# Mixer and expert block: VectorE's turned rows, up's clip and glu put together behind the first low part of the down row

## The chip, the cores and the metric

The kernel is one program on one core of a Trainium2 chip. What is measured is the device time of one execution, in microseconds (us), the median of the runs shown. The core has TensorE (matmuls and transposes through the matrix unit), VectorE (called DVE in the profile), ScalarE (ACT), GpSimd (POOL) and SyncE (SP), which here only issues the loads. Each runs its own list of instructions in order and waits on semaphores for the others.

## The reference

Two blocks stand one behind the other, with 512 tokens of width 1024. The first is a mixer (an mLSTM in chunks and a pooling branch), then a layer of 32 experts, of which each token uses four. The second is a stick-breaking attention with spatial gating. The change touches the experts alone:

```python
logits = (xt @ w_router + b_router).astype(jnp.float32)
top_vals, top_idx = lax.top_k(logits, TOP_K)          # 4 of 32
top_gates = jax.nn.softmax(top_vals, axis=-1)
...
def expert_block(args):
    xb, e = args                                       # rows of one expert
    gate = xb @ w_gate[e] + b_gate[e]                  # 1024 x 1024
    up = xb @ w_up[e] + b_up[e]                        # 1024 x 1024
    gate = jnp.minimum(gate, SWIGLU_LIMIT)             # 7
    up = jnp.clip(up, -SWIGLU_LIMIT, SWIGLU_LIMIT)
    glu = gate * jax.nn.sigmoid(SWIGLU_ALPHA * gate)
    return (glu * (up + 1.0)) @ w_down[e] + b_down[e]  # 1024 x 1024
...
y_buf = y_buf * gate_buf[:, None]
out = jax.ops.segment_sum(y_buf, tok_buf, num_segments=T + 1)[:T]
```

## The kernel before, in words

**Places.** The experts are taken in an order found at run time, one behind the other at 32 places e = 0 to 31. At even places there is room for 128 rows, at odd places (`small(e)`) for 64; what is over would be done in a loop afterwards.

**High and low parts.** Products are kept near float32 by splitting both factors: the high part is the value rounded to the matmul's format, the low part is the rest, and high by high, high by low and low by high are summed. For weights ScalarE writes the high part (`high`, L1062: `WH` from the landing place `ring` or `land`), and VectorE subtracts it from the landed value (`low`, L1408: `low` or `WL`). A low part is written over the place that the weights landed in; ten places are shared so. For the rows of an expert the high parts are `xh` (gathered rows, turned) and `hh` (glu, turned), the low parts `xl` and `hl`. At an odd place the low part lies in the other half of `xh` or `hh`, so that one matmul of 128 columns multiplies both with the high weights, and the lower half of the result is added to the upper one by a fold (L789), after ScalarE has copied it (`egl` for the gate, `eul` L1215 for up, `ysl` for the output).

**Groups.** A matrix of weights comes in four pieces of 1 MB. Each piece is one group of matmuls on TensorE (`rows_by_columns`): 24 matmuls of 512 columns at an even place, 16 at an odd one. There are five buffers for high parts, so ScalarE can make the high part of piece n only when TensorE is done with piece n - 5, and the ten places let SyncE load piece n when TensorE is done with piece n - 10. `ahead(n)` is n + 4: in the step of piece n, ScalarE and VectorE make the parts of piece n + 4.

**What is done at place e, in TensorE's order.** `tensor_gate_up(e)`: four groups of gate and four of up; before the last three of them, behind group 4, comes `tensor_index(e + 3)`, a product of the one-hots of place e + 3 (`oh`, L1703 on VectorE) that gives which rows this expert has. Then `tensor_turn_rows(e + 1)` (L775, `PS<-C,xg`): the gathered rows of the next place are turned into PSUM banks 6 and 7. Then `tensor_down(e - 1)`: the four groups of the down weights of the place before (the down row of this text). Then `tensor_turn_mid(e)` (L775, `PS<-C,eu`): the glu of place e is turned into the same banks 6 and 7. It waits for the glu (`s_eh`) and for the low part of the next rows (`s_tl`), since that reads these banks.

**VectorE at place e.** During gate and up: the low part of the weights in each of eight steps; in step 1 the low part of the glu turned before (`hh` or `hl`); in step 2 the one-hots of place e + 3 (L1703); in step 5 the index of place e + 3 (three short instructions, L1709 to L1713, `iv`, `dst`, `tok`). During the down row: four low parts of weights and three instructions more, `vector_up` (L1730, up's clip, `eu`), `vector_glu` (L1736, (up + 1) times the gate's part, `eu`), and `vector_turn8` (L1720 `xl` or L1718 `xh`, the low part of the next rows). Where these three stand is what the change alters.

**ScalarE at place e.** The high parts of the weights, the high part of the turned rows (`scalar_turn8`, L1206 and L1204), the gate's clip and gelu (L1231, L1233), the copies for the folds and the output `ys` (L1243). GpSimd gathers the rows of place e + 2 and scatters the output of place e - 1; SyncE issues one load of 1 MB a piece.

All of these orders are written out by hand in loops; no planner is at work.

Of the kernel before, what the change touches and what calls it, by code (L numbers as in the profile page):

```python
# [15 lines left out]
T, D, E, K = 512, 1024, 32, 4  # L16
# [57 lines left out]
def program(nc, x, norm1_g, w_in, ig_b, fg_b, conv_w, head_norm_g, pool_w, pool_scale, w_out, norm2_g,  # L74
# [51 lines left out]
    def reg(name, shape, dt, kb):  # L126
        return place(name, shape, dt, off=R0 + int(kb * KB))
# [77 lines left out]
    xh = reg("xh", [128, 8, 128], F32R, 8)  # L205
    xl = reg("xl", [128, 8, 128], F32R, 12)
# [228 lines left out]
    t_rows = {e: max(0, 2 * e - 1) for e in range(E)}  # L435
    t_mid = {e: 2 * e + 2 if e + 1 < E else 2 * e + 1 for e in range(E)}
    NI = 3
    small = lambda e: e % 2 == 1
# [11 lines left out]
    def ahead(n):  # L450
        return n + 2 if n >= second else min(n + NX - 1, second - 1) if n >= first else min(n + 2, first)
# [602 lines left out]
    def high(upto):  # L1054

        while state["hi"] <= min(upto, NP - 1):
            n = state["hi"]
            state["hi"] += 1
            A.wait_ge(s_land[spot[n]], landed(n))
            if before[n]:  # L1060
                A.wait_ge(s_mm, before[n])
            A.activation(WH[buf[n]], lands[spot[n]], ACT.Copy).then_inc(s_hi, 1)  # L1062
# [138 lines left out]
    def scalar_turn8(t, o, e):  # L1201
        A.wait_ge(s_tt, t + 1)
        if small(e):
            A.activation(o[:, :, 0:HALF], PS[:, 6, :].rearrange("p (k t) -> p k t", k=8), ACT.Copy).then_inc(s_th, 1)  # L1204
        else:
            A.activation(o, PS[:, 6:8, :].rearrange("p h (k t) -> p (h k) t", k=4), ACT.Copy).then_inc(s_th, 1)  # L1206

    def scalar_gate_low(e):
        A.wait_ge(s_mm, done[n_g[e] + 4])
        A.wait_ge(s_eh, e)  # L1210
        A.activation(egl[HALF:128], PS[HALF:128, 0:2, :], ACT.Copy).then_inc(s_low, 1)

    def scalar_up_low(e):
        A.wait_ge(s_mm, done[n_g[e] + 8])
        A.activation(eul[HALF:128], PS[HALF:128, 2:4, :], ACT.Copy).then_inc(s_low, 1)  # L1215

    def scalar_out_low(e):
        A.wait_ge(s_mm, done[n_d[e] + 4])
        A.activation(ysl[HALF:128], PS[HALF:128, 4:6, :], ACT.Copy).then_inc(s_low, 1)

    def scalar_gate(e):
        n = places(e)
        if small(e):
            A.wait_ge(s_fold, fold["gate", e])
        else:
            A.wait_ge(s_mm, done[n_g[e] + 4])
        if e:
            A.wait_ge(s_eh, e)
        else:
            A.wait_ge(s_sp, 1)  # L1230
        A.activation(eg[0:n], PS[0:n, 0:2, :], ACT.Relu, scale=-1.0, bias=C[0:n, LIM:LIM + 1]).then_inc(s_eg, 1)  # L1231
        A.wait_ge(s_eg, e + 1)
        A.activation(eg[0:n], eg[0:n], ACT.Gelu_apprx_sigmoid, scale=-1.0, bias=C[0:n, LIM:LIM + 1]).then_inc(s_es, 1)  # L1233

    def scalar_out(e):
        n = places(e)
        if e >= 2:
            A.wait_ge(s_y[e % 2], 16 * (e // 2))
        if small(e):
            A.wait_ge(s_fold, fold["out", e])  # L1240
        else:
            A.wait_ge(s_mm, done[n_d[e] + 4])
        A.activation(ys[e % 2][0:n], PS[0:n, 4:6, :], ACT.Copy).then_inc(s_ys, 1)  # L1243

    def scalar_experts():
        A.wait_ge(s_h2, 64)
        high(first + NX - 1)
        scalar_turn8(0, xh, 0)
        for e in range(E + 1):
            if e < E:  # L1250
                for p in range(8):
                    if p == 0 and small(e) and e >= 3:
                        scalar_out_low(e - 2)
                    if p == 4 and small(e):
                        scalar_gate_low(e)
                    high(ahead(n_g[e] + p))
                    if p == (2 if small(e) else 0) and e >= 2:
                        scalar_out(e - 2)
                    if p == 1 and e:
                        scalar_turn8(t_mid[e - 1], hh, e - 1)  # L1260
                    if p == (6 if small(e) else 4):
                        scalar_gate(e)
                    if p == 6 and e == 1:
                        A.wait_ge(s_spt, 1)
                        A.activation(GtT, PS[0:32, 6, :].rearrange("p (j t) -> p j t", j=4), ACT.Copy).then_inc(s_spk, 1)
            else:
                scalar_out(E - 2)
                scalar_turn8(t_mid[E - 1], hh, E - 1)
            for p in range(4):
                if p == 0 and small(e):  # L1270
                    scalar_up_low(e)
                if e:
                    high(ahead(n_d[e - 1] + p))
                if p == 1 and e + 1 < E:
                    scalar_turn8(t_rows[e + 1], xh, e + 1)
        scalar_out_low(E - 1)
        scalar_out(E - 1)
# [122 lines left out]
    def low(upto):  # L1400

        while state["lo"] <= min(upto, NP - 1):
            n = state["lo"]
            state["lo"] += 1
            V.wait_ge(s_hi, n + 1)
            if second <= n < second + NS:
                V.wait_ge(s_mm, low_free[n])
            V.tensor_tensor(WLn[n], lands[spot[n]], WH[buf[n]].bitcast(F32), SUB).then_inc(s_lo, 1)  # L1408
# [271 lines left out]
    def vector_positions():  # L1680
        V.wait_ge(s_pos, 2)
        V.wait_ge(s_m16, 2)
        V.scalar_tensor_tensor(P1, PS[:, 4, 0:128].rearrange("p (j e) -> p j e", j=4), 1.0, M16, ADD, MUL).then_inc(dv.sem, dv.one())
        V.tensor_copy(cnt, PS[:, 4, 128:160]).then_inc(dv.sem, dv.one())
        V.wait_ge(dv.sem, dv.n)
# [29 lines left out]
    def vector_turn8(t, hi, lo, e):  # L1715
        V.wait_ge(s_th, t + 1)
        if small(e):
            V.tensor_tensor(hi[:, :, HALF:128], PS[:, 6, :].rearrange("p (k t) -> p k t", k=8), hi[:, :, 0:HALF].bitcast(F32), SUB).then_inc(s_tl, 1)  # L1718
            return
        V.tensor_tensor(lo, PS[:, 6:8, :].rearrange("p h (k t) -> p (h k) t", k=4), hi.bitcast(F32), SUB).then_inc(s_tl, 1)  # L1720
# [11 lines left out]
    def vector_glu(e):  # L1732
        V.wait_ge(s_eu, e + 1)
        V.wait_ge(s_es, e + 1)
        n = places(e)
        V.scalar_tensor_tensor(eu[0:n], eu[0:n], 1.0, eg[0:n], ADD, MUL).then_inc(s_eh, 1)  # L1736

    def vector_experts():
        V.wait_ge(s_xg[0], 16)
        low(first + 2)  # L1740
        vector_turn8(0, xh, xl, 0)
        vector_positions()
        for q in range(1, NI):
            vector_one_hot(q)
        low(first + 3)
        vector_further_count()
        V.wait_ge(s_ek, 1)
        V.reciprocal(sm, sm).then_inc(dv.sem, dv.one())
        V.wait_ge(dv.sem, dv.n)
        V.tensor_tensor(GK, GK, sm.unsqueeze(2).broadcast_to([128, 4, 4]), MUL).then_inc(s_gk, 1)  # L1750
        V.wait_ge(s_gk, 1)
        spread_out(Gt, GK).then_inc(s_sp, 1)
        low(first + NX - 1)
        for e in range(E + 1):
            if e < E:
                for p in range(8):
                    if e or p < 7:
                        low(ahead(n_g[e] + p))
                    if e == 0 and p + 1 < NI:
                        vector_index(p + 1, 4 + p)  # L1760
                    if p == 1 and e:
                        vector_turn8(t_mid[e - 1], hh, hl, e - 1)
                    if p == 2 and e + NI < E:
                        vector_one_hot(e + NI)
                    if p == 5 and e + NI < E:
                        vector_index(e + NI, 7)
            else:
                vector_turn8(t_mid[E - 1], hh, hl, E - 1)
            if e == 0:
                vector_turn8(t_rows[1], xh, xl, 1)  # L1770
                vector_up(0)
                vector_glu(0)
                low(ahead(n_g[0] + 7))
                continue
            for p in range(4):
                low(ahead(n_d[e - 1] + p))
                if e < E and p == (1 if small(e) else 0):
                    vector_up(e)
                if e < E and p == 1 and small(e):
                    vector_glu(e)  # L1780
                if e + 1 < E and p == 1:
                    vector_turn8(t_rows[e + 1], xh, xl, e + 1)
                if e < E and p == 1 and not small(e):
                    vector_glu(e)

    def vector_join():
# [482 lines left out]
    scalar_heads()  # L2269
    scalar_routing()  # L2270
    scalar_experts()
    vector_mixer()
    vector_heads()
# [39 lines left out]
```

## Time and profile before

| | |
|---|---|
| time, median of 3 runs | 1762.07 us (1759.75 to 1762.36) |
| profiled execution | 1760.04 us, its span 1758.7 us |
| mean granted TensorE clock | 0.985 of full speed |
| TensorE busy (matmuls) | 1668.6 us, 95% of the span, 7609 matmuls |
| VectorE busy | 1376.8 us, 78% |
| ScalarE busy | 1207.5 us, 69% |
| GpSimd busy | 246.6 us, 14% |
| all weight high parts (L1062, two groups) | 210 x 1911 ns and 218 x 1912 ns |
| weight low parts (L1408, the two large groups) | 194 x 2282 ns and 190 x 2282 ns |
| a load of 1 MB, from issue to landing | 7.6 to 8.3 us, the medians of the experts' six kinds |

The page divides the span into 40 slices of 44 us. The experts take the time from about 235 us to about 1310 us. In these slices the page has TensorE, VectorE and nearly always ScalarE at 8 or 9 tenths, and the memory at 390 to 410 GB/s; before and behind them VectorE and ScalarE have less to do. Busy shares say who has little slack. Who waits for whom stands in the list of waits and, place by place, in the timeline. In the timeline a start and a length stand ahead of the engine; in brackets stands how long the engine had been idle and what it waited for. Matmuls overlap, so that the modelled end of one group lies a little behind the start of the next.

### The profile page before, as it was taken

To read this page: it belongs to the slowest core of one execution; us is meant where nothing else is said; L and a number is where in the kernel's file an instruction comes from. 1 tells how busy PE (TensorE), PEld (TensorE's weight loads), DVE (VectorE), ACT (ScalarE), POOL (GpSimd) and SP (SyncE) were. 2 spreads that over 40 slices of the span, in tenths; PEclk is the share of its full clock that TensorE was granted. 3 is DMA by queue.
4 is the path that set the end of the run, shared out by engine and by line. 5 is a ranking of instruction groups with operands and counts; after the bars stand their busy time and mean duration, and the time that the engine had idled before them with its cause. 6 is when DMAs were issued, how large, how long until landed. Compare 5 with 4: busy or idle time off the path is not lost.

```text
span 1758.7 us, 19816 instructions
## 1 busy us (share of the span) xinstructions
PE 1668.6 (95%) x7609; PEld 1249.1 (71%) x7609; DVE 1376.8 (78%) x1226; ACT 1207.5 (69%) x931; POOL 246.6 (14%) x143
## 2 busy tenths in 40 slices
PE   7999979999999999999999999999979999999998
PEld 5877857676676676676676676676754877778887
DVE  4576689999999999999999999999957324865343
ACT  4344458889889889879888889889863347564232
POOL 1402041111111111210210210212110000000000
PEclk9999989999999999999999999999988999999999
DMA  7312479999999999999999999999956221212221
GB/s 281 129 48 74 130 268 360 386 406 402 388 397 401 389 393 404 390 391 403 388 390 401 390 388 405 384 388 411 388 194 262 96 72 48 72 55 96 96 84 48
DMA packets 94000, 487.96 MB, mean 277 GB/s; under 512 B 12056, under 2 KB 13776, under 8 KB 43984
## 3 DMA queue, kind: packets, MB, share of 16 engines
q1 hardware_dynamic: 81696, 462.64, 67.7%
q0 software_dynamic: 8000, 18.25, 2.9%
q10 hardware_dynamic: 4208, 5.77, 1.0%
q8 instruction: 62, 1.02, 0.2%
q14 instruction: 34, 0.28, 0.0%
HBM read 477.97 MB, written 17.17 MB: 282 GB/s over the span
## 4 chain that ended last, share of the span: by engine, by line
PE 72%; DVE 16%; issue 6%; ACT 5%; DMA 1%; SPq 0%; DVEq 0%; ACTq 0%; POOLq 0%
PE PS L536 64%; DVE low L1408 5%; DVE WL L1408 5%; ACT WH L1062 3%; PE PS L775 2%; PE PS L997 1%; DVE eu L1730 1%; DVE eu L1736 1%; PE PS L1009 1%; PE PS L789 1%; DVE hl L1720 1%; DVE oh L1703 1%; DVE xh L1718 1%; DMA h2d<-HV 0%; PE PS L648 0%
## 5 line engine op out<-in xcount | busy, mean ns | idle before, releaser
L1062 ACT ACTIVATE WH<-land 128x2048 fp32r<-128x2048 f32 x210 | 398.6, 1911 | 150.8 <-PE PS L536 150.3
L1062 ACT ACTIVATE WH<-ring 128x2048 fp32r<-128x2048 f32 x218 | 414.0, 1912 | 94.7 <-PE PS L536 87.9
L1408 DVE TENSOR_TENSOR low<-ring,WH 128x2048 fp32r<-128x2048 f32 x194 | 437.3, 2282 | 24.1 <-ACT WH L1062 24.0
L1408 DVE TENSOR_TENSOR WL<-land,WH 128x2048 fp32r<-128x2048 f32 x190 | 428.3, 2282 | 26.8 <-ACT WH L1062 26.8
L536 PE MATMUL PS<-WH,xh 128*128 128x512 f32 x1024 | 307.5, 402 | 2.2 <-DVE xh L1718 1.5
L2061 POOL DMA_INDIRECT yd<-ys,dst x32 | 107.3, 3355 | 860.4 <-ACT ys L1243 860.4
L536 PEld LDWEIGHTS PS<-WH,xh 128*128 128x128 f32 x1024 | 187.0, 189 | 52.3 <-issue 7.3
L536 PE MATMUL PS<-WH,hh 128*128 128x512 f32 x512 | 154.8, 404 | 3.8 <-DVE hh L1718 3.8
L536 PE MATMUL PS<-low,xh 128*128 128x512 f32 (+1 forms) x520 | 151.7, 395 | 0.0
L536 PE MATMUL PS<-WL,xh 128*128 128x512 f32 (+1 forms) x504 | 146.7, 395 | 0.0
L536 PE MATMUL PS<-WH,xl 128*128 128x512 f32 x512 | 137.7, 391 | 0.0
L1408 DVE TENSOR_TENSOR WL<-ring,WH 128x2048 fp32r<-128x2048 f32 x24 | 54.7, 2288 | 99.7 <-ACT WH L1062 99.7
L536 PEld LDWEIGHTS PS<-WH,hh 128*128 128x128 f32 x512 | 93.6, 190 | 32.1 <-issue 5.3
L536 PE MATMUL PS<-h,WH 128*128 128x512 f32 x288 | 113.3, 394 | 0.0
L536 PE MATMUL PS<-l,WH 128*128 128x512 f32 x288 | 112.2, 390 | 0.0
L536 PEld LDWEIGHTS PS<-WH,xl 128*128 128x128 f32 x512 | 96.7, 189 | 20.7
L536 PEld LDWEIGHTS PS<-low,xh 128*128 128x128 f32 (+1 forms) x520 | 82.6, 162 | 35.9 <-issue 4.2
L536 PEld LDWEIGHTS PS<-WL,xh 128*128 128x128 f32 (+1 forms) x504 | 79.8, 162 | 35.6 <-issue 4.4
L1408 DVE TENSOR_TENSOR low<-land,WH 128x2048 fp32r<-128x2048 f32 x20 | 45.7, 2288 | 49.3 <-ACT WH L1062 49.3
L2049 POOL DMA_INDIRECT xg<-h2d,tok x32 | 79.9, 2496 | 28.0 <-DVE tok L1713 16.2
L536 PE MATMUL PS<-low,hh 128*64 128x512 f32 (+1 forms) x256 | 74.4, 399 | 0.0
L536 PE MATMUL PS<-WL,hh 128*128 128x512 f32 (+1 forms) x256 | 73.6, 391 | 0.0
(399 smaller groups left out, 2616.9 us busy)
## 6 DMA issues: line engine op xcount, KB each, us to landing
ring<-in_w_gate_dram SPq DMA_DIRECT2D x66, 1024.0 KB, 7.6
ring<-in_w_up_dram SPq DMA_DIRECT2D x64, 1024.0 KB, 8.3
land<-in_w_up_dram SPq DMA_DIRECT2D x64, 1024.0 KB, 8.0
land<-in_w_down_dram SPq DMA_DIRECT2D x64, 1024.0 KB, 8.1
ring<-in_w_down_dram SPq DMA_DIRECT2D x64, 1024.0 KB, 8.2
land<-in_w_gate_dram SPq DMA_DIRECT2D x62, 1024.0 KB, 8.0
ring<-in_w_in_dram SPq DMA_DIRECT2D x19, 1024.0 KB, 5.7
land<-in_w_in_dram SPq DMA_DIRECT2D x13, 1024.0 KB, 5.3
```

The lines of the kernel that those rows point to most:

```text
L536: return P.matmul(ps, a, b, start=start, stop=stop)
L775: last = P.transpose(PS[:, 6 + at_ // 512, at_ % 512:at_ % 512 + n], pairs_[0:n, k // 2, k % 2], ident[0:n, 0:n])
L789: last = P.matmul(PS[0:HALF, b0 + hf, :], foldw[HALF:128], lows[HALF:128, hf], start=False, stop=True, skip_group_check=True)
L997: last = P.matmul(flat[:, OFF[i] + 128 * (i2 - i):OFF[i] + 512 - 128 * i], tri[:, 0 if i2 == i else 1], part[:, OFF[i2]:OFF[i2] + 512 - 12 ...
L1009: last = P.matmul(flat[:, OFF[i]:OFF[i] + 512 - 128 * i], kT[r0:r0 + 64, ch, 128 * i:128 * i + 128], nq[r0:r0 + 64, ch, 128 * i:512], star ...
L1062: A.activation(WH[buf[n]], lands[spot[n]], ACT.Copy).then_inc(s_hi, 1)
L1408: V.tensor_tensor(WLn[n], lands[spot[n]], WH[buf[n]].bitcast(F32), SUB).then_inc(s_lo, 1)
L1703: last = V.tensor_scalar(oh[q % NI][:, j, 0:n], iot16[:, 0:n], P1[:, j, q:q + 1], None, ALU.is_equal)
L1718: V.tensor_tensor(hi[:, :, HALF:128], PS[:, 6, :].rearrange("p (k t) -> p k t", k=8), hi[:, :, 0:HALF].bitcast(F32), SUB).then_inc(s_tl, 1)
L1720: V.tensor_tensor(lo, PS[:, 6:8, :].rearrange("p h (k t) -> p (h k) t", k=4), hi.bitcast(F32), SUB).then_inc(s_tl, 1)
L2049: G.indirect_dma_start(xg[i][0:n], None, h2d, bass.IndirectOffsetOnAxis(tok[0:n, e:e + 1], 0), bounds_check=T - 1, oob_is_err=False).then_ ...
L2061: G.indirect_dma_start(yd, bass.IndirectOffsetOnAxis(dst[0:n, e:e + 1], 0), ys[e % 2][0:n].rearrange("p h f -> p (h f)"), None, bounds_che ...
```

## The change

On VectorE, in the down row of place e, three instructions are now made behind the first low part: the low part of the next rows, up's clip, glu, in this order, at even and at odd places alike. Before, an even place had the clip behind the first low part and the rows' low part and the glu behind the second; an odd place had clip, glu and rows behind the second. On ScalarE the high part of the next rows, from which VectorE subtracts, is made behind the first high part of the down row, before behind the second. The number of instructions is the same on each engine, and TensorE, GpSimd and SyncE keep their order. Ten shared places were there before.

```diff
@@ scalar_experts, in the loop over the down row's steps p
                 if e:
                     high(ahead(n_d[e - 1] + p))
-                if p == 1 and e + 1 < E:
+                if p == 0 and e + 1 < E:
                     scalar_turn8(t_rows[e + 1], xh, e + 1)
@@ vector_experts
             for p in range(4):
                 low(ahead(n_d[e - 1] + p))
-                if e < E and p == (1 if small(e) else 0):
+                if e < E and p == 0:
+                    if e + 1 < E:
+                        vector_turn8(t_rows[e + 1], xh, xl, e + 1)
                     vector_up(e)
-                if e < E and p == 1 and small(e):
-                    vector_glu(e)
-                if e + 1 < E and p == 1:
-                    vector_turn8(t_rows[e + 1], xh, xl, e + 1)
-                if e < E and p == 1 and not small(e):
                     vector_glu(e)
```

VectorE in the down row of an even place: L1408 is a low part of weights (the number behind a name is the buffer), L1730 up's clip, L1736 the glu, L1718 the low part of the next, odd, place's rows.

```order
 L1408 TENSOR_TENSOR low_249<-ring_51,WH_56 128x2048
 L1408 TENSOR_TENSOR low_250<-ring_52,WH_57 128x2048
-L1730 TENSOR_SCALAR eu<-PS 128x1024
-L1408 TENSOR_TENSOR low_251<-ring_53,WH_175 128x2048
-L1718 TENSOR_TENSOR xh<-PS,xh 128x8x64
-L1736 SCALAR_TENSOR_TENSOR eu<-eu,eg 128x1024
+L1718 TENSOR_TENSOR xh<-PS,xh 128x8x64
+L1730 TENSOR_SCALAR eu<-PS 128x1024
+L1736 SCALAR_TENSOR_TENSOR eu<-eu,eg 128x1024
+L1408 TENSOR_TENSOR low_251<-ring_53,WH_175 128x2048
 L1408 TENSOR_TENSOR low_252<-ring_54,WH_176 128x2048
 L1408 TENSOR_TENSOR WL_59<-land_244,WH_58 128x2048
```

The second low part of the row moved behind the three others, and the rows' low part ahead of the clip, so that clip and glu now stand together.

VectorE in the down row of an odd place: the same, with 64 rows in the clip and the glu, and L1720 as the low part of the next, even, place's rows.

```order
 L1408 TENSOR_TENSOR WL_178<-land_248,WH_176 128x2048
 L1408 TENSOR_TENSOR low_253<-ring_55,WH_58 128x2048
-L1408 TENSOR_TENSOR low_249<-ring_51,WH_56 128x2048
-L1730 TENSOR_SCALAR eu<-PS 64x1024
-L1736 SCALAR_TENSOR_TENSOR eu<-eu,eg 64x1024
-L1720 TENSOR_TENSOR xl<-PS,xh 128x1024
+L1720 TENSOR_TENSOR xl<-PS,xh 128x1024
+L1730 TENSOR_SCALAR eu<-PS 64x1024
+L1736 SCALAR_TENSOR_TENSOR eu<-eu,eg 64x1024
+L1408 TENSOR_TENSOR low_249<-ring_51,WH_56 128x2048
 L1408 TENSOR_TENSOR low_250<-ring_52,WH_57 128x2048
 L1408 TENSOR_TENSOR low_251<-ring_53,WH_175 128x2048
```

The second low part moved behind the three others, and the rows' low part from the end of them to their head.

ScalarE around the down row of an even place, before: L1062 is a high part of weights, L1204 the high part of the next rows, L1219 the copy for the fold.

```order
L1062 ACTIVATE WH_57<-ring_52 128x2048
L1062 ACTIVATE WH_175<-ring_53 128x2048
L1204 ACTIVATE xh<-PS 128x8x64
L1062 ACTIVATE WH_176<-ring_54 128x2048
L1062 ACTIVATE WH_58<-land_244 128x2048
L1219 ACTIVATE ysl<-PS 64x1024
```

And ScalarE at the same place in the changed kernel.

```order
L1062 ACTIVATE WH_57<-ring_52 128x2048
L1204 ACTIVATE xh<-PS 128x8x64
L1062 ACTIVATE WH_175<-ring_53 128x2048
L1062 ACTIVATE WH_176<-ring_54 128x2048
L1062 ACTIVATE WH_58<-land_244 128x2048
L1219 ACTIVATE ysl<-PS 64x1024
```

The high part of the rows went ahead of the second high part of the row, and nothing else moved.

## Rows read from the trace of the kernel before

**Rows 1.** Waits of the whole run: engine, line, waited for: total us, times, longest

```profile
PE PS L536 <- DVE oh L1703: 19.6, 15, 2.0
...
PE PS L775 <- DVE eu L1736: 11.6, 15, 0.8
```

**Rows 2.** Timeline of VectorE, 853 to 885: start, length, instruction, [idle before]

```profile
856.75 2.29 DVE L1408 TENSOR_TENSOR low<-ring,WH 128x2048 fp32r<-128x2048 f32 x1 [0.42 <-ACT WH L1062]
858.96 1.22 DVE L1730 TENSOR_SCALAR eu<-PS 128x1024 f32<-128x1024 f32 x1
860.10 2.28 DVE L1408 TENSOR_TENSOR WL<-land,WH 128x2048 fp32r<-128x2048 f32 x1
...
862.90 1.21 DVE L1736 SCALAR_TENSOR_TENSOR eu<-eu,eg 128x1024 f32<-128x1024 f32 x1
864.03 8.89 DVE L1408 TENSOR_TENSOR WL<-land,WH 128x2048 fp32r<-128x2048 f32 x4
...
876.17 0.90 DVE L1703 TENSOR_SCALAR oh<-iot,P 128x128 f16<-128x128 f16 x4
...
883.80 0.15 DVE L1713 TENSOR_SCALAR tok<-dst 128x1 int32<-128x1 int32 x1
```

**Rows 3.** Timeline of TensorE's matmuls, 853 to 885

```profile
853.64 1.07 PE L536 MATMUL PS<-WH,xl 128*128 128x512 f32 x4
854.64 1.17 PE L775 MATMUL PS<-C,xg 64*128 64x64 f32 x8
...
862.30 1.09 PE L536 MATMUL PS<-WH,hh 128*128 128x512 f32 x4
864.16 1.23 PE L775 MATMUL PS<-C,eu 128*128 128x128 f32 x8 [0.77 <-DVE eu L1736]
...
867.08 1.08 PE L536 MATMUL PS<-WL,xh 128*64 128x512 f32 x4
...
877.22 0.24 PE L536 MATMUL PS<-DV,oh 128*128 128x1 f16 x4 [1.31 <-DVE oh L1703]
...
884.06 1.20 PE L775 MATMUL PS<-C,xg 128*128 128x128 f32 x8 [0.28 <-issue]
```

**Rows 4.** Timeline of ScalarE, 853 to 885

```profile
854.80 1.92 ACT L1062 ACTIVATE WH<-ring 128x2048 fp32r<-128x2048 f32 x1 [0.80 <-PE PS L536]
857.94 1.92 ACT L1062 ACTIVATE WH<-land 128x2048 fp32r<-128x2048 f32 x1 [1.22 <-PE PS L536]
859.77 0.57 ACT L1204 ACTIVATE xh<-PS 128x512 fp32r<-128x512 f32 x1
```

**Rows 5.** Timeline of all engines, 826 to 832, an odd place

```profile
826.79 1.21 DVE L1730 TENSOR_SCALAR eu<-PS 64x1024 f32<-64x1024 f32 x1
...
828.03 1.22 DVE L1736 SCALAR_TENSOR_TENSOR eu<-eu,eg 64x1024 f32<-64x1024 f32 x1
...
829.17 1.21 DVE L1720 TENSOR_TENSOR xl<-PS,xh 128x1024 fp32r<-128x1024 f32 x1
829.37 1.07 PE L536 MATMUL PS<-WH,hl 128*128 128x512 f32 x4
...
830.53 1.14 PE L775 MATMUL PS<-C,eu 64*128 64x64 f32 x8
```

**Rows 6.** Timeline of all engines, 1200 to 1230, the last places

```profile
1200.19 1.92 ACT L1062 ACTIVATE WH<-land 128x2048 fp32r<-128x2048 f32 x1 [0.40 <-PE PS L536]
...
1219.49 0.68 PE L789 MATMUL PS<-eul,foldw 64*64 64x512 f32 x2 [0.72 <-ACT eul L1215]
...
1229.56 1.14 PE L775 MATMUL PS<-C,eu 64*128 64x64 f32 x8 [0.98 <-DVE xl L1720]
```

**Rows 7.** Timeline of TensorE after two of its longer idles

```profile
1299.15 2.04 PE L536 MATMUL PS<-WH,hh 128*128 128x512 f32 x4 [3.77 <-DVE hh L1718]
...
1350.06 1.09 PE L568 MATMUL PS<-C,HG 128*128 128x128 f32 x8 [2.02 <-DVE HG L1815]
```

**Rows 8.** Engines by stretch: bounds, length, busy (instructions), clock, DMA share, GB/s

```profile
1300.00:1304.00 4.00, 4.00 (x11) 2.18 (x11) 0.00 (x0) 0.00 (x0) 0.00 (x0) 0.50 0.13 54
```

## The prediction

> **What bounds the kernel now.** I read the waits of the whole run first, since TensorE has the highest busy share of the table. In the experts TensorE waits for two things worth a count: 15 times for the one-hots (L1703), 19.6 us together, and 15 times for the glu (L1736), 11.6 us [rows 1]. The change makes the glu earlier, so the first thought is a gain of some 11 us. Then I followed one pair of places in time, to see whether a wait that goes stays gone. Take the even place whose row of down weights begins at 856 us.
>
> VectorE last sits idle before 856.75 (0.42 us, for ScalarE's copy). From there to the row's end at 883.80, the last step of the place index, no row has an idle bracket [rows 2]: 27.2 us, to 883.95, of gapless work. TensorE stands three times on things that this stretch makes: 0.77 us on the glu at 864.16, 1.31 us on the one-hots at 877.22, and 0.28 us on the index at 884.06, 0.11 us after it is written [rows 3]. From 884.06 TensorE runs through the odd place's down row and the whole gate and up of the next even place. The last group of these, ending 853.64 + 1.07 = 854.71 a pair earlier [rows 3], lets ScalarE make the copy at 854.80 [rows 4], which VectorE takes up at 856.75. So a pair of places takes a TensorE stretch (884 to 855 of the next pair), a handover, and a VectorE stretch of 27.2 us. The glu's wait lies beside the VectorE stretch, not in TensorE's.
>
> **Even places, the order.** VectorE from 856.75 did low, up's clip, low, low part of the rows, glu. Start to start the first low takes 858.96 - 856.75 = 2.21 us, the clip 860.10 - 858.96 = 1.14, the second low and the turn together 862.90 - 860.10 = 2.80 (so the turn is 0.60 beside a low of 2.20), the glu 864.03 - 862.90 = 1.13 [rows 2]. Now it is low, turn, clip, glu, low. The glu reads what the clip wrote. Where they already stand together, at an odd place, they are 828.03 - 826.79 = 1.24 us apart [rows 5], 0.10 more than the 1.14 with another instruction between. So: turn at 858.96, clip 859.56, glu 860.80, ending 862.01; second low from 861.93 to about 864.2, where it used to end at 862.38.
>
> TensorE's down row ends at 862.30 + 1.09 = 863.39 [rows 3], so the glu no longer holds it. A turn whose wait is long over starts 0.07 before the modelled end of the work ahead of it (854.64 against 854.71) [rows 3], so TensorE starts at 863.32 and is 864.16 - 863.32 = 0.84 us ahead. It gives this back at the one-hots: VectorE's work before them is the same plus 0.10, and they wait now for 1.31 + 0.84 + 0.10 = 2.25 us. Gain 0, cost 0.10 a pair. The one-hots are made at odd places 3 to 27, 13 pairs: 13 x 0.10 = +1.3 us.
>
> What else moves there: ScalarE's copy of the rows (0.57 us) goes ahead of the second weight copy, into the 1.22 us in which ScalarE waits for TensorE [rows 4]. The gathered rows are turned by 854.64 + 1.17 = 855.81, the copy would run 856.72 to 857.29, and VectorE wants it at 858.96, 1.67 us later. Without that cover the copy's 0.57 us would lengthen VectorE's stretch. The second low part is wanted first by the group that starts at 867.08, now 866.24 at the earliest; it is ready at 864.2, 2.0 us before. Loads are asked for when TensorE has used a place, so they shift with it and no wait is added on their queue; the same holds for GpSimd, whose gathers wait for the index, whose time stays.
>
> The Trainium skill speaks against my 0.10 ("VectorE: DVE Perf Modes", section "The DRAIN you can't avoid"): a semaphore between two VectorE instructions costs nothing extra. The distances 1.24 and 1.14 disagree with it here. By it the term of 1.3 us would be nothing.
>
> **Odd places.** VectorE did low, low, clip, glu, turn; now low, turn, clip, glu, low. TensorE's turn of the glu waits there for the low part of the rows too. That ended at 829.17 + 1.21 = 830.38 and TensorE starts at 830.53, though its group before ended at 829.37 + 1.07 = 830.44 [rows 5]: +0.09 where a free start is -0.07, so 0.16 us is lost. With a low (2.20) taken from in front of them all, glu and rows are ready about 2 us before. This is in TensorE's stretch, so it stays: 13 x 0.16 = -2.1 us. Bounds: 0 (it is TensorE's own delay) and 0.16.
>
> **The last pairs.** From place 29 on there are no one-hots to make and nothing takes back the 0.84. ScalarE is the one that TensorE meets then: at 1200.19 it waits 0.40 us for TensorE, and later TensorE waits 0.72 us for its copy eul (L1215), and 0.98 us for the rows' low part xl [rows 6]. With TensorE 0.84 ahead and ScalarE's copy of the rows made early, that chain is 0.84 us earlier, and the 0.98 goes too, with the 0.07: 0.84 + 1.05 = 1.9 us. The last even place (30) does it once more into 31, 0.84 us. Together -2.7 us; bounds 1.05 (ScalarE does not follow) and 2.7.
>
> **Sum.** +1.3 - 2.1 - 2.7 = -3.5 us. The profiled execution took 1760.04 us, so 1756.5 by its own time; the median of the three runs is 2.03 us above that, so 1762.07 - 3.5 = 1758.6 us. Its own ends: terms at their best (0, -2.1, -2.7) 1757.3, at their worst (+1.3, 0, -1.05) 1762.3; the runs of before lie up to 2.3 us under their median. So 1755 to 1762.5 for this case.
>
> **Rivals.**
> A. All is kept: the one-hots' wait is not VectorE's gapless work, and the glu's 15 x 0.84 = 12.6 us come off beside 2.1 and 1.05. 1762.07 - 15.8 = 1746.3 us. For it: the wait is real and 15 times there. Against it: not one idle bracket between 856.75 and 883.80 [rows 2]. Chance 0.10.
> B. The dependent pair costs nothing, by a closer look at VectorE's own pacing: -2.1 - 2.7 = -4.8, 1757.3 us. This is what the skill's rule above gives. Chance 0.12.
> C. Nothing comes of the odd places or the last ones, since TensorE's 0.09 us are its own and ScalarE holds the end: +1.3 us, 1763.4 us. Chance 0.12.
> D. Slower: the granted clock falls. TensorE's idle at the one-hots grows from 1.31 to 2.25 us. After an idle of 3.77 us four matmuls took 2.04 us instead of the 1.09 of the same four at 862.30 [rows 3, 7], and the stretch behind was granted 0.50, the lower level of 1.2 GHz [rows 8]; after 2.02 us of idle the eight transposes took 1.09 us, shorter than the 1.17 at 854.64 [rows 3, 7]. So it decides somewhere between 2.02 and 3.77, and 2.25 is near the safe end. Price: half of 4.0 us and of the 0.85 before, 2.4 us; 0.35 of each lies in TensorE's slack ahead of 884.06. 13 x 2.05 = 27, less the 3.5: 1785 us. Chance 0.06.
> The skill's page "TensorE: Matmul & The Clock Gate", Part 1, says that idling halves the clock and sustained work restores it. The trace agrees, with 0.50 after the 3.77 us.
>
> **Chances.** Forecast 0.60, A 0.10, B 0.12, C 0.12, D 0.06. A measurement of this kernel can tell about 0.2%, 3.5 us, from no change: a line at 1758.55, right at my forecast. Faster: A, B's 0.10, and a little under half of the forecast, 0.25: 0.45. Same: the other half 0.34, C's 0.11 and 0.02 of B, 0.47. Slower 0.08: D, and 0.02 of the worst ends. The range for 8 in 10 takes in the forecast's own, B and C, and a little beyond each: 1753.5 to 1763.5.
>
> **What would show it.** On VectorE the order low, turn, clip, glu, low, with 0.10 more between clip and glu at even places; on TensorE no wait for L1736, but 13 waits for L1703 of about 2.25 us instead of 1.31; a pair of places as long as before within 0.1 us; at 1200 us and later the eul and xl waits shorter. I am wrong if the one-hots' wait does not grow (A), if VectorE has a new idle bracket before its turn (ScalarE's copy late), or if the granted clock dips once a pair (D).

## The result, and the profile after

The changed kernel takes 1766.14 us, median of 7 runs (1764.85 to 1767.68), beside 1761.22 us before (7 runs). The ratio is 1.0027, 95% interval 1.0018 to 1.0037: slower by some 5 us, outside my range of 1753.5 to 1763.5 us, where I had forecast 3.5 us less. The profiled execution took 1764.85 us (span 1763.5), that of before 1760.04 us (1758.7).

The page has a first sign only in sums and means: for the same 7609 matmuls TensorE was busy 1668.6 us before and is 1676.0 now, and its mean granted clock was 0.985 before and is 0.976 now. The row of clocks in 40 slices is 9 throughout the experts in both kernels (slices 11 to 26), since a digit 9 stands for all from 90% up, and a slice of 44 us hides 3 us at half.

```profile
PE 1676.0 (95%) x7609; PEld 1258.8 (71%) x7609; DVE 1377.3 (78%) x1226; ACT 1208.4 (69%) x931; POOL 316.9 (18%) x143
...
PEclk9999979999999999999999999999997999999999
```

The same stretch of the experts in both kernels, the columns as in [rows 8]. First before, where the clock (third figure from the right) is full:

```profile
432.00:1164.00 732.00, 704.98 (x3234) 513.37 (x3234) 696.12 (x507) 629.14 (x408) 126.12 (x44) 1.00 1.00 394
```

Then after:

```profile
432.00:1164.00 732.00, 703.68 (x3198) 515.87 (x3198) 689.25 (x502) 622.35 (x403) 180.67 (x44) 0.98 0.99 390
```

In the waits of the whole run, what answers to [rows 1]: the wait for the glu (L1736) is gone altogether, and the one for the one-hots went from 19.6 to 34.9 us.

```profile
PE PS L536 <- DVE oh L1703: 34.9, 15, 2.5
```

VectorE at the same even place as in [rows 2], which begins at 863.13 here and not at 856.75 (6.4 us later, by what had been lost until then):

```profile
863.13 2.29 DVE L1408 TENSOR_TENSOR low<-ring,WH 128x2048 fp32r<-128x2048 f32 x1 [0.42 <-ACT WH L1062]
...
865.34 0.68 DVE L1718 TENSOR_TENSOR xh<-PS,xh 128x512 fp32r<-128x512 f32 x1
...
865.94 1.22 DVE L1730 TENSOR_SCALAR eu<-PS 128x1024 f32<-128x1024 f32 x1
...
867.19 1.23 DVE L1736 SCALAR_TENSOR_TENSOR eu<-eu,eg 128x1024 f32<-128x1024 f32 x1
...
868.33 11.09 DVE L1408 TENSOR_TENSOR WL<-land,WH 128x2048 fp32r<-128x2048 f32 x5
...
882.67 0.91 DVE L1703 TENSOR_SCALAR oh<-iot,P 128x128 f16<-128x128 f16 x4
...
890.31 0.15 DVE L1713 TENSOR_SCALAR tok<-dst 128x1 int32<-128x1 int32 x1
```

The order is low, turn, clip, glu, low, with no idle bracket up to the index. The glu starts 1.25 us behind the clip whose output it reads; an instruction that read nothing of the clip's started 1.14 us behind it. From the start of the first low to the one-hots it takes 19.54 us, before 876.17 - 856.75 = 19.42. ScalarE at the same place, what answers to [rows 4]; its copy of the rows is done well before VectorE's turn at 865.34:

```profile
861.18 1.92 ACT L1062 ACTIVATE WH<-ring 128x2048 fp32r<-128x2048 f32 x1 [0.80 <-PE PS L536]
...
863.00 0.58 ACT L1204 ACTIVATE xh<-PS 128x512 fp32r<-128x512 f32 x1
```

TensorE there, what answers to [rows 3]:

```profile
868.67 1.09 PE L536 MATMUL PS<-WH,hh 128*128 128x512 f32 x4
...
869.61 1.11 PE L775 MATMUL PS<-C,eu 128*128 128x128 f32 x8
...
883.73 0.24 PE L536 MATMUL PS<-DV,oh 128*128 128x1 f16 x4 [2.50 <-DVE oh L1703]
...
890.57 1.20 PE L775 MATMUL PS<-C,xg 128*128 128x128 f32 x8 [0.28 <-issue]
```

The glu no longer holds its turn, and the idle ahead of the one-hots is 2.50 us. From 883.73 to the turn of the rows it takes 6.84 us, as before, and the next one-hots follow 66.55 us later, as before (66.57). That is a pair in which nothing changed. The pair ahead of it looked like this from its one-hots on:

```profile
816.10 0.24 PE L536 MATMUL PS<-DV,oh 128*128 128x1 f16 x4 [2.50 <-DVE oh L1703]
...
817.16 1.59 PE L536 MATMUL PS<-WH,xh 128*128 128x512 f32 x4
818.55 1.91 PE L536 MATMUL PS<-WL,xh 128*64 128x512 f32 x4
820.25 1.40 PE L536 MATMUL PS<-WH,xh 128*128 128x512 f32 x4
```

The groups of four that take 1.08 us elsewhere take 1.59, 1.91 and 1.40 us. From the one-hots (816.10) to the turn (824.09) it is 7.99 us instead of 6.84, and the pair is 67.63 us long. The clock in these 3 us is half, which is the level of 1.2 GHz (a slow stretch, from here on):

```profile
818.00:821.00 3.00, 3.00 (x8) 1.89 (x8) 3.00 (x2) 1.91 (x1) 0.00 (x0) 0.51 1.05 343
```

I took the starts of all one-hot products at odd places 3 to 27 from both timelines. Before: the 12 distances between these 13 are 66.56 to 66.60 us, and from every one it is 6.84 us to the turn. After: 9 of 13 have 7.9 to 8.0 us to the turn, and the distances are 66.6 us (after a product without a slow stretch) or 67.6 to 67.7 us (with one). The first of the 13 starts at 344.65 and 344.86, the last at 1143.50 and 1152.13. So of the 4.8 us in the span +0.2 arise ahead of these pairs and +8.4 in them, in 8 slow stretches of some 1.06, and from the last one-hots to the end the changed kernel is 3.8 us faster, with the ninth slow stretch in it.

### The profile page after: what moved, and what is told of

Read it like the earlier page. It is cut to its first block, busy times and chain, and to the rows that moved or that the text cites. A ratio compares the mean times of both kernels' runs of the same rounds, so it can differ in the third digit from the quotient of the medians.

```text
span 1763.5 us, 19816 instructions
## 1 busy us (share of the span) xinstructions
PE 1676.0 (95%) x7609; PEld 1258.8 (71%) x7609; DVE 1377.3 (78%) x1226; ACT 1208.4 (69%) x931; POOL 316.9 (18%) x143
## 3 DMA queue, kind: packets, MB, share of 16 engines
q1 hardware_dynamic: 81696, 462.64, 67.6%
## 4 chain that ended last, share of the span: by engine, by line
PE 73%; DVE 17%; ACT 6%; issue 3%; DMA 1%; SPq 0%; DVEq 0%; ACTq 0%; POOLq 0%
PE PS L536 65%; DVE low L1408 6%; DVE WL L1408 5%; ACT WH L1062 3%; PE PS L775 2%; PE PS L997 1%; PE PS L1009 1%; DVE eu L1736 1%; PE PS L789 1%; DVE eu L1730 1%; DVE hl L1720 1%; DVE oh L1703 1%; DVE xh L1718 1%; PE PS L648 0%; DMA ring<-in_w_in_dram 0%
## 5 line engine op out<-in xcount | busy, mean ns | idle before, releaser
L1062 ACT ACTIVATE WH<-land 128x2048 fp32r<-128x2048 f32 x210 | 398.2, 1912 | 147.4 <-PE PS L536 146.9
L1062 ACT ACTIVATE WH<-ring 128x2048 fp32r<-128x2048 f32 x218 | 413.9, 1913 | 98.9 <-PE PS L536 92.6
L1408 DVE TENSOR_TENSOR low<-ring,WH 128x2048 fp32r<-128x2048 f32 x194 | 436.9, 2283 | 26.9 <-ACT WH L1062 26.9
L1408 DVE TENSOR_TENSOR WL<-land,WH 128x2048 fp32r<-128x2048 f32 x190 | 427.9, 2284 | 29.4 <-ACT WH L1062 29.4
L536 PE MATMUL PS<-WH,xh 128*128 128x512 f32 x1024 | 314.6, 410 | 2.2 <-DVE xh L1718 1.5
L2058 POOL DMA_INDIRECT yd<-ys,dst x32 | 142.5, 4454 | 795.6 <-ACT ys L1243 795.6
L536 PEld LDWEIGHTS PS<-WH,xh 128*128 128x128 f32 x1024 | 192.0, 194 | 54.7 <-issue 8.9
L536 PE MATMUL PS<-WL,xh 128*128 128x512 f32 (+1 forms) x504 | 151.0, 405 | 0.0
L1408 DVE TENSOR_TENSOR WL<-ring,WH 128x2048 fp32r<-128x2048 f32 x24 | 54.8, 2289 | 99.0 <-ACT WH L1062 99.0
L2046 POOL DMA_INDIRECT xg<-h2d,tok x32 | 114.9, 3592 | 27.0 <-DVE tok L1713 15.2
L1408 DVE TENSOR_TENSOR low<-land,WH 128x2048 fp32r<-128x2048 f32 x20 | 45.7, 2288 | 49.3 <-ACT WH L1062 49.3
```

The source lines that it names most:

```text
L536: return P.matmul(ps, a, b, start=start, stop=stop)
L2046: G.indirect_dma_start(xg[i][0:n], None, h2d, bass.IndirectOffsetOnAxis(tok[0:n, e:e + 1], 0), bounds_check=T - 1, oob_is_err=False).then_ ...
L2058: G.indirect_dma_start(yd, bass.IndirectOffsetOnAxis(dst[0:n, e:e + 1], 0), ys[e % 2][0:n].rearrange("p h f -> p (h f)"), None, bounds_che ...
```

## The experiments

All times below are medians; the ratio is to the kernel before, run beside it, with its 95% interval.

**The new order at odd places alone.**

```diff
-                if p == 1 and e + 1 < E:
+                if p == (0 if small(e) else 1) and e + 1 < E:
                     scalar_turn8(t_rows[e + 1], xh, e + 1)
...
+                if small(e):
+                    if e < E and p == 0:
+                        if e + 1 < E:
+                            vector_turn8(t_rows[e + 1], xh, xl, e + 1)
+                        vector_up(e)
+                        vector_glu(e)
+                else:
...
```

> The new order at odd places alone, for VectorE and ScalarE; even places as before. Theory (the changed kernel is slower because TensorE's longer idle ahead of the one-hots, 2.50 us instead of 1.31, lets its granted clock fall at even-odd pairs): here the idle stays 1.3 us, no dip, the mean clock stays 0.985, the turn of the glu at odd places loses its 0.16 us 13 times (2.1 us) and place 29 its wait for xl (1.0 us): about 1758, 3 us less than before. Rival (the new order itself is slower on VectorE or ScalarE, wherever it stands): slower than before, by about half of the 5 us, 1763.

1757.56 us, ratio 0.9983 (0.9974 to 0.9992). All 12 distances between the one-hot products are 66.43 to 66.45 us, 0.14 less than before, with the idle at 1.31 and no slow stretch. The odd half of the change is a small gain: 3.0 us by the medians, where 2.1 and 1.0 had been worked out.

**The new order at even places alone** (the same edit with `not small(e)`).

> The new order at even places alone. Theory of the clock: the idle ahead of the one-hots is 2.5 us, in about 9 of 13 pairs the clock falls to half and costs 1.1 us each (9.7 us), 13 x 0.12 us for the dependent clip and glu, less some 3 us at the last places: about 1769, mean clock 0.976. Rival: half of the loss, 1763, the clock no part of it.

1779.91 us, ratio 1.0115 (1.0099 to 1.0130): a loss of 19 us where some 8 had been expected. TensorE there:

```profile
823.15 0.24 PE L536 MATMUL PS<-DV,oh 128*128 128x1 f16 x4 [2.50 <-DVE oh L1703]
...
844.62 1.14 PE L775 MATMUL PS<-C,eu 64*128 64x64 f32 x8 [0.60 <-DVE xl L1720]
```

And the stretch behind the one-hots:

```profile
823.00:826.00 3.00, 2.85 (x13) 1.96 (x14) 3.00 (x3) 1.57 (x2) 0.01 (x1) 0.75 1.04 436
826.00:831.00 5.00, 5.00 (x18) 3.05 (x17) 4.93 (x6) 3.46 (x3) 0.00 (x0) 0.81 1.00 326
```

The 0.75 of the first 3 us and the 0.81 of the next 5 are some 1.5 and 2 us at half, in one piece. The idle is 2.50 us again, and here the clock fell in 13 of 13 pairs (8.0 us from every product to the turn). Each pair takes 68.29 us. Of the 1.72 us more, 1.15 lie between the one-hots and the turn; the rest is the 0.12 of the dependent glu and a wait for xl at odd places that was 0.16 and is 0.60 now, since VectorE comes out of the slow stretch late. All of the loss is in this half of the change. The rival of a loss shared by both halves falls.

**Fillers in the idle.** The changed kernel with eight transposes of the identity ahead of the wait; nobody reads them. Lines behind the insert have numbers 3 higher (L1706 is L1703).

```diff
             if p == 4:
                 P.wait_ge(s_tl, t_mid[e - 1] + 1 if e else 1)
+                if small(e) and e + NI < E:
+                    for k in range(8):
+                        P.transpose(PS[:, 7, 128 * (k % 4):128 * (k % 4) + 128], ident, ident)
                 if e + NI < E:
                     tensor_index(e + NI, 7)
```

> The changed kernel with eight transposes of the identity (about 1.1 us) on TensorE at odd places ahead of its wait for the one-hots, into a part of the bank that nobody reads. Nothing else moves. Theory of the clock: the idle is cut from 2.5 to about 1.3 us, the dips go, a pair takes 66.6 us everywhere: 1766.1 - 9.7 = 1756.4 us, mean clock 0.985. Rival (loads, GpSimd's longer DMA issues, or the order itself): the filler lies in idle time and changes nothing, 1766.

1754.11 us, ratio 0.9962 (0.9948 to 0.9975), 12.0 us under the changed kernel.

```profile
877.47 1.04 PE L877 MATMUL PS<-C 128*128 128x128 f32 x8
880.04 0.25 PE L536 MATMUL PS<-DV,oh 128*128 128x1 f16 x4 [1.53 <-DVE oh L1706]
...
881.10 1.08 PE L536 MATMUL PS<-WH,xh 128*128 128x512 f32 x4
```

The idle is 1.53 us, the groups behind it take 1.08 us, and the 12 distances are 66.55 to 66.57 us. More work on TensorE made the kernel faster, and the slow stretches are gone with it, while the order on the other engines and of the loads is the changed kernel's. By the rival (the loads, GpSimd or the order itself) the time would have stayed at 1766. A filler shortens the idle and adds work ahead of it; which of the two keeps the clock is not told apart. GpSimd's busy time in 432 to 1164 us was 126 us before, 181 after and 136 here; the fastest kernel below has the most, 261 in 698 us, so it doesn't set the time.

**Fillers in the kernel before.** The profile of the last one had TensorE standing 0.38 us at the branch behind the experts, 3.5 us before and 3.9 us in the changed kernel, so part of the 12.0 us might have been that.

> The kernel before with the same eight filler transposes. Its idle of 1.31 us shrinks to about 0.3 and its pairs stay 66.57 us. In the changed kernel with fillers TensorE stood 0.38 us instead of 3.5 to 3.9 us at the branch behind the experts, with nothing waited for. Theory: that comes of the few instructions more on TensorE (where its code lies) and not of the clock or the order: here too it is about 0.4 instead of 3.5 us, and the time 3.1 us under before, 1757.5. Rival (it comes with the new order): 3.5 us again, 1760.6.

1756.28 us, ratio 0.9977 (0.9967 to 0.9986).

```profile
1315.26 13.92 PE L536 MATMUL PS<-bd,GtT 32*128 32x512 f32 x16 [0.38 <-issue]
```

The idle at the branch is 0.38 us here too. In the four kernels with filler instructions it is 0.4 to 0.5 us, in the eight without 3.4 to 3.9 us. (Ahead of the one-hots the idle is 0.35 us here, and the pairs take 66.5 us, 0.08 less than before, where I had expected no change.) So 3.1 to 3.5 us of what the fillers won is not the clock in the pairs. The two profiled executions, of the changed kernel and of the same with fillers, are 10.7 us apart: 8.6 between the first and the last of the 13 products, which are the slow stretches, and 4.8 behind them (3.5 at the branch), while the stretch ahead of them is 2.7 longer with fillers. That stretch varies without fillers too: the first of the 13 starts at 344.65 before and at 347.47 with the new order at odd places alone. So the 8.6 us are the clock's, and the 12.0 us as a whole are not. Nor is the branch all that is shorter: from its first matmuls to the end it takes 441.1 and 441.3 us in the two kernels with eight fillers and 443.8 before, for a reason that wasn't looked for.

Against this kernel as base, the changed order without slow stretches is worth 0.0015 of the time, 2.6 us, but the two intervals overlap, and the profile of this kernel has a slow stretch of its own, behind the wait for xl at place 29:

```profile
1231.65 1.14 PE L775 MATMUL PS<-C,eu 64*128 64x64 f32 x8 [0.97 <-DVE xl L1723]
```

```profile
1234.00:1238.00 4.00, 4.00 (x13) 3.15 (x12) 4.00 (x2) 0.56 (x1) 3.60 (x1) 0.65 0.81 336
```

**Two and four fillers,** to set the idle at other lengths.

> As the kernel with eight filler transposes, but two of them, so that TensorE's idle ahead of the one-hots is about 2.26 us: what my forecast had worked out (2.25), where the changed kernel has 2.50. It asks whether the forecast's idle would have kept the clock. If the fall decides by the idle alone and above 2.3 us: no dips, about 1756 to 1757. If 2.26 is enough for it: dips in most pairs, 1764 or more.

1762.03 us, ratio 1.0009 (1.0000 to 1.0018). The idle is 2.19 us, and 9 of 13 pairs have a slow stretch, one of them here:

```profile
816.60 0.25 PE L536 MATMUL PS<-DV,oh 128*128 128x1 f16 x4 [2.19 <-DVE oh L1706]
816.72 1.92 PE L536 MATMUL PS<-WL,xh 128*64 128x512 f32 x4
818.43 1.89 PE L536 MATMUL PS<-WH,xh 128*128 128x512 f32 x4
```

> The changed kernel with four filler transposes: TensorE's idle ahead of the one-hots about 1.95 us, between the 2.19 us of two of them (9 of the 12 longer pairs dipped) and the 1.53 us of eight (none). If the dips need about 2 us of idle: none or few, about 1755 us. If they are as many as at 2.19: 1762.

1760.47 us (1754.27 to 1763.60), ratio 0.9994 (0.9982 to 1.0006). The idle is 1.97 us, and 6 of 13 pairs have a slow stretch: neither of the two outcomes, but a share between. Both kernels also have the shorter wait at the branch, 0.48 us, so their times are some 3 us lower than the slow stretches alone would make them. Every such count is of one profiled execution. That of this kernel took 1757.67 us, and its 12 runs lie 9.3 us apart, so the share may well differ from run to run.

**The new order from place 28 on alone** (the same edit with `e >= 28`).

> The new order from place 28 on alone, the places behind which no one-hots are waited for; before them everything as before. Theory: the gain of the changed kernel at its end, 4.9 us from the last one-hots to the end of the run by its profile, comes alone, without the dips: 1761.2 - 4.9 = 1756.3 us. My forecast's own term for the last places was 2.7 us: 1758.5. Rival (the gain there is a phase or DMA effect of what came before): no change, 1761.

1757.92 us, ratio 0.9985 (0.9976 to 0.9994): 2.7 us under before, the forecast's term for the last places (the interval is 1.1 to 4.2 us). The 4.9 us read from the changed kernel's profile (3.8, and 1.07 for the ninth slow stretch) were too much; the profile of this one has 3.1 us from the last one-hots to the end.

**The one-hots a row earlier.** To find what a pair is held by once the clock is seen, the changed kernel with

```diff
-                    if p == 2 and e + NI < E:
+                    if p == 2 and e <= 1 and e + NI < E:
                         vector_one_hot(e + NI)
...
                     vector_up(e)
                     vector_glu(e)
+                    if e + 1 + NI < E:
+                        vector_one_hot(e + 1 + NI)
```

> The changed kernel, with the one-hots of the next place's index made on VectorE right behind the glu, a gate row earlier than now (from place 2 on). The work on VectorE is the same, and its stretch is still gapless to the index (three short instructions in step 5). Theory (VectorE's gapless stretch is what holds a pair, not the one-hots themselves): the wait for the one-hots goes and comes back whole as a wait for the index ahead of turning the rows, about 2.7 us; a pair takes 66.5 us or more with a dip, so 1764 to 1767. Rival A (the one-hots' wait is the price): it goes, 13 x 2.5 us, 1730.

1774.79 us, ratio 1.0080 (1.0066 to 1.0094). TensorE:

```profile
892.51 1.09 PE L536 MATMUL PS<-WH,xh 128*128 128x512 f32 x4
896.06 1.39 PE L775 MATMUL PS<-C,xg 128*128 128x128 f32 x8 [2.46 <-issue]
897.11 1.20 PE L536 MATMUL PS<-WH,hh 128*128 128x512 f32 x2
```

VectorE:

```profile
895.81 0.15 DVE L1713 TENSOR_SCALAR tok<-dst 128x1 int32<-128x1 int32 x1
```

The wait for the one-hots is gone and comes back as 2.46 us in one piece ahead of the turn, 0.10 us behind VectorE's index. Two matmuls behind it take 1.20 us instead of 0.70, and 11 of the 12 distances are 68.0 to 68.2 us (the other is 66.6). The theory of the gapless stretch held in its place. I had not counted on a slow stretch in nearly each pair, so the time is 8 us above what I expected. The rival (1730) falls.

**And the index a step earlier.**

```diff
-                    if p == 5 and e + NI < E:
+                    if p == 4 and e + NI < E:
                         vector_index(e + NI, 7)
```

> The same and the index one step earlier (behind the low part of step 4 instead of 5), so that both things that TensorE waits for come 2.2 to 2.9 us earlier in VectorE's stretch, ahead of a low part that is not wanted so soon. Theory: both waits nearly go, no idle is long enough for a dip, TensorE becomes gapless but for 0.2 to 0.5 us a pair and a pair takes about 64.2 us: 1756.4 (the changed kernel without dips) less 13 x 2.3 = 1726 us. If the low parts or the loads of 1 MB (the memory is at 390 GB/s now and would be asked for 404) become the bound, less: 1740.

1729.90 us (1727.75 to 1731.63), ratio 0.9824 (0.9810 to 0.9837), 30 us under before and 4 us over what was expected: the version that beats both kernels. VectorE at an even place and the odd one behind it:

```profile
844.82 0.74 DVE L1703 TENSOR_SCALAR oh<-iot,P 128x128 f16<-128x128 f16 x4
845.47 11.10 DVE L1408 TENSOR_TENSOR WL<-land,WH 128x2048 fp32r<-128x2048 f32 x5
...
864.59 0.15 DVE L1713 TENSOR_SCALAR tok<-dst 128x1 int32<-128x1 int32 x1
```

TensorE's turn of the rows there:

```profile
864.85 1.20 PE L775 MATMUL PS<-C,xg 128*128 128x128 f32 x8 [0.23 <-issue]
```

And the experts as a whole:

```profile
432.00:1130.00 698.00, 693.19 (x3184) 504.40 (x3183) 685.27 (x497) 620.09 (x402) 261.46 (x44) 1.00 1.01 407
```

A pair takes 64.36 us, TensorE is busy 693 of 698 us at full clock, and the memory gives 407 GB/s. In the pairs TensorE waits for neither one-hots nor glu; ScalarE now waits for ten of the loads' landings, up to 1.1 us each.

**The same two moves with the old order of the row.**

> The kernel before (old order of the row) with the one-hots made behind the glu of the place before and the index in step 4. It asks what the changed order is worth once the waits behind it are gone. Theory: TensorE's wait for the glu at even places (0.77 us and the 0.07 and 0.1 around it) and for xl at odd places (0.16 us) now lie bare: a pair takes 64.36 + 1.1 = 65.5 us, so about 1730 + 14 = 1744 us, and the order that cost 0.27% alone is worth 0.8% here. Rival (the order is worth nothing in either): 1730.

1769.17 us (1765.83 to 1773.63), ratio 1.0050 (1.0036 to 1.0065). TensorE has the waits that the new order takes away, for the glu and for xl:

```profile
865.79 1.23 PE L775 MATMUL PS<-C,eu 128*128 128x128 f32 x8 [0.77 <-DVE eu L1736]
...
898.33 1.14 PE L775 MATMUL PS<-C,eu 64*128 64x64 f32 x8 [0.99 <-DVE xl L1720]
```

And behind such a wait for xl, in another pair:

```profile
965.00:970.00 5.00, 5.00 (x18) 4.05 (x18) 5.00 (x3) 1.45 (x2) 2.75 (x1) 0.66 0.97 405
```

Of the 12 distances 7 are 66.2 us and the five others 67.8: the clock, 0.66 in these 5 us, falls here too, behind an idle of 0.98 us. The profile has seven such falls, all behind waits for xl of 0.98 to 1.01 us, two of them behind the last product. I had expected 65.5 a pair and 1744 us, with 0.16 us for the wait for xl, which came out at 0.99. With these moves the changed order is worth some 39 us. The two profiled executions are 35.4 us apart: 12 x 1.8 us are the two waits (0.77 and 0.99), some 11 us the seven slow stretches of 1.6.

## Why the prediction was wrong

- **Even places, where the glu's gain goes.** Right: the wait for the glu went, VectorE's stretch stayed gapless, and TensorE gave all back at the one-hots. The idle there was mis-sized: 2.50 us for 2.25. TensorE reached the turn 0.93 us earlier and not 0.84 (7.49 us from the start of its down row at 862.12 to 869.61; before 864.16 - 855.74 = 8.42), its work behind the turn began 0.13 sooner (0.86 us after the turn's start for 0.99), and VectorE's cost was 0.12.
- **The dependent pair, 0.10 us.** Right: 0.12 us, in every pair. Rival B did not hold. The rule behind it in the Trainium skill ("VectorE: DVE Perf Modes", section "The DRAIN you can't avoid"), that a semaphore between two VectorE instructions costs nothing extra, disagrees with the rows here: 867.19 - 865.94 = 1.25 us for the dependent pair, 1.13 to 1.14 us for the clip and a follower that reads nothing of it. Whether the semaphore or the reading costs it isn't told apart.
- **Odd places, -2.1 us.** Right: with the new order at odd places alone the pairs are 0.14 us shorter, 1.8 us in 13. What answers to [rows 5] in the changed kernel:

```profile
902.45 1.07 PE L536 MATMUL PS<-WH,hl 128*128 128x512 f32 x4
...
903.45 1.17 PE L775 MATMUL PS<-C,eu 64*128 64x64 f32 x8
```

  The turn starts 0.07 before the modelled end of the group, and no longer 0.09 behind it.
- **The last places, -2.7 us.** Right, measured alone as 2.7 us. That the wait for eul would be shorter was wrong: it went from 0.72 to 0.86 us. What answers to [rows 6]; the wait for xl is gone:

```profile
1228.07 0.68 PE L789 MATMUL PS<-eul,foldw 64*64 64x512 f32 x2 [0.86 <-ACT eul L1215]
...
1237.07 1.17 PE L775 MATMUL PS<-C,eu 64*128 64x64 f32 x8
```

- **The step that failed: the fall of the clock, which stands at nothing in the sum and had a chance of 0.06 as rival D.** It measured nine falls of 1.07 us, 9.6 us in all. The mechanism was on my list, with its place and the right sign, and I set it aside with the words that it "decides somewhere between 2.02 and 3.77, and 2.25 is near the safe end". It decides by more than one number. At idles of 2.50, 2.19, 1.97 and 1.53 us in the same place the clock fell in 9, 9, 6 and 0 of 13 pairs, and with another spacing of the pairs at 2.50 in 13 of 13. Two rows, one with a fall and one without, bounded nothing. The changed kernel itself shows it: its idle at the very place of my row without a fall, at 2.03 us, was followed by one, at a mean clock of 0.60 in the 4 us from there.

```profile
1356.46 1.67 PE L568 MATMUL PS<-C,HG 128*128 128x128 f32 x8 [2.03 <-DVE HG L1812]
```

```profile
1356.00:1360.00 4.00, 3.54 (x11) 2.46 (x12) 3.93 (x4) 1.11 (x3) 0.00 (x0) 0.60 0.02 3
```

  Ten of the twelve kernels have this idle of 2.02 to 2.03 us, and in three of them the clock fell behind it. My row without a fall was one draw.
- **Its price** was wrong the other way: 1.07 us a time and not 2.05, because the slow stretch was about 3 us long and not 5. Had the forecast had the fall in 9 of 13, at 1.07 us, it would have read -3.5 + 9.6 = +6.1 us; measured were +4.9.

What stays open: why the clock falls in one pair and not in the next, at the same idle. Nor was it tried whether the falls behind waits of 1 us need the other waits near them.

## What to carry to other kernels

An idle of TensorE that "costs nothing", because what comes behind it is waited for anyway, can cost the clock: two short waits (0.8 and 1.3 us) were cheaper than one of 2.5 us, and even useless matmuls put into that one paid. When a wait is removed ahead of a gapless stretch of another engine, first ask which instruction at that stretch's end TensorE waits for, and move that one too: the same edit was 0.3% slower alone and with the one-hots and the index moved it was 1.8% faster. One row without an effect doesn't bound an effect that comes in part of the cases.

## What the runs showed of the hardware that I had not expected

- The granted clock fell to half for some 3 us behind idles of 1.97 to 2.50 us, in 6 to 13 of 13 like places, behind one of 2.02 to 2.03 us in three kernels of ten, and behind waits of 0.97 to 1.01 us seven times in one kernel and once in another; at the one-hots, behind 1.31 us (three kernels) and 1.53 us (one), it never did in 13 pairs.
- At the branch behind the experts TensorE stood 3.4 to 3.9 us in eight kernels and 0.4 to 0.5 us in the four that had 2 to 8 instructions more in each odd place, with no wait named in either. The wait is 3 us shorter so; the cause (where the code lies is a guess) wasn't tried by itself.
- Two VectorE instructions of which the second reads the first's output start 0.11 us further apart (1.25 us) than two that don't depend on each other (1.14 us).
